# A delta-rule scan on one core: each projection issued in two pieces instead of four

## Chip, cores and metric

One core of one Trainium2 chip runs the whole program. The metric is device time in microseconds, the median of the runs shown. Lower is better. All data is float32.

## What is computed

The program is a pair of transformer-like blocks over 512 tokens of width 1024. The part at issue is the first block's RWKV-7 mixer: the input is projected, shifted along time by three taps, turned into per-head quantities, and scanned forward and backward with a delta rule, first over 256 context tokens, then over the 512 tokens themselves. Cut to that part, the reference is:

```python
z = h @ p["w_in"]
r, k_f, k_b, v, d_f, d_b, kk, a_f, a_b, dg = rwkv_prep(centred_shift(z_rwkv, p["shift_conv"]), p)

def centred_shift(z, w):
    zp = jnp.pad(z, ((0, 0), (1, 1), (0, 0)))
    return zp[:, :-2] * w[0] + zp[:, 1:-1] * w[1] + zp[:, 2:] * w[2]

def step(S, inp):                                  # rwkv_scan, 16 heads of 64
    r_t, k_t, v_t, d_t, kk_t, a_t = inp
    s_kk = jnp.einsum('bhvk,bhk->bhv', S, kk_t)
    S_new = (S * d_t[:, :, None, :] - s_kk[..., None] * (kk_t * a_t)[:, :, None, :]
             + v_t[..., None] * k_t[:, :, None, :])
    y = jnp.einsum('bhvk,bhk->bhv', S if reverse else S_new, r_t)
    return S_new, y
```

After it come the rest of the mixer (merge), a mixture-of-experts layer, and a second block. They take some two thirds of the time and are not touched.

## The kernel before

`stage_scan` (L552) works on eight column groups j = 0..7 of 128 columns, that is two heads each. The scan is chunked: 12 steps of 64 tokens (4 of the context, 8 of the tokens), both directions side by side. Each step needs the inverse of a triangular matrix; the inverses are made in three groups s = 0, 1, 2 of four steps, each by LEVELS = 5 levels l of block doubling. All engines' orders are written out by hand and run in order; semaphores tie them together. The outer loop is over turns j = -1..8. In a turn the engines make the inverses of column group j, run the sequential steps of j (and in s = 0 those last four of j-1), and in the time left prepare the column group b = j+1 and finish a = j-1.

One level (s, l) of a turn on PE, L1083 to L1105, is in this order:

- product (L810, beside it read-outs of values L959, keys L933, or turned tokens L795): DVE then makes the mask (L1445) of its result
- if l < 4, the right side of a step (L904, L908): ACT then negates it (`negate`, L1173)
- half-slot 0: `beside(j, (s, l, 0))`
- if l < 4, the solve (L920), which waits for the negation. ACT then copies U (`solved`, L1179)
- the correct (L880, L882), which waits for the mask; at l = 4 correct_last (L862, L865) stands instead. DVE then updates X and XT (L1456, L1458)
- if l < 4, the read out (L945), which waits for the copy of U. DVE then makes the next state (L1471, L1475)
- half-slot 1: `beside(j, (s, l, 1))`. The next level's product waits for the update.

Each half-slot is named by three numbers, (s, l, 0) or (s, l, 1). `beside` on PE, L1000 to L1078, says which work of b or a goes into each. ACT, DVE have such functions too, with the same names of slots: on ACT the work of half-slot 0 stands between the negation and the copy of U, on DVE that of half-slot 0 between mask and update, that of half-slot 1 behind the state.

`project(j, which, piece)` (L694) makes one of four projections of a column group, by matmuls from `hT` and the weights in `first_chunk`, into one PSUM bank, PROJ: K_X (keys of the tokens), K_V (keys and values of the context, two outputs of 256 columns, L710), R_X and V_X (512 columns, L714), each summed over eight blocks c of 128 rows. A projection is cut into four pieces: two blocks c of 512 columns, or four of 256. In the trace a float32 matmul has two records, so a piece shows as x4 (L714) or x8 (L710). PROJ is one bank: a projection waits until DVE's `shift` (L1484, three operations, at L376, L379, L382 for X and from L1500 on for the context) has read the one before, and the shift of each waits for its last piece (semaphore `proj`).

Work of ACT that stands in half-slots 0 and matters here: at (1,0,0) tokens and `deviation` (L1287, L1292) of column a; at (1,3,0) tokens and `part_moved` (L1229); at (2,0,0) tokens and `blend` (L1259); at (2,3,0) `part_moved` and `exponents` (L1266 to L1270). On DVE: `shift(b, K_X)` at (0,2,1), K_V at (1,1,1), R_X at (2,1,0), V_X at (2,4,1), the last followed by `scaled_q`; `unit_k` (L1553) at (2,0,1). GpSimd (POOL) has `new_k` (L1391 to L1393) after the blend.

Of the kernel before, what the change touches and what calls it, by code (L numbers as in the profile page):

```python
# [12 lines left out]
T, TC, D = 512, 256, 1024  # L13
TA = T + TC
KT = D // P
# [536 lines left out]
def stage_scan(k, hT, th, da, sg, ya, spare, m, first_chunk, first_loaded):  # L552
# [20 lines left out]
    with ExitStack() as s:  # L573
# [40 lines left out]
        Y, RU, INV, INVT, PROJ = (bank[i] for i in range(5))  # L614
# [22 lines left out]
        K_X, K_V, R_X, V_X = range(4)  # L637
# [22 lines left out]
        def _(pe):  # L660
# [33 lines left out]
            def project(j, which, piece):  # L694

                if not live(j):
                    return
                if piece == 0:
                    if which == K_X:
                        pe.wait_ge(S["wk_loaded"], 16 * (j + 1))  # L700
                    elif which == R_X:
                        pe.wait_ge(S["wr_loaded"], 16 * (j + 1))
                    elif which == K_V:
                        pe.wait_ge(S["wv_loaded"], 16 * (j + 1))
                    if proj_no(j, which) > 1:
                        pe.wait_ge(S["shift"], shift_no(j, which - 1) if which else shift_no(j - 1, V_X))
                if which == K_V:
                    i, o = (1, PROJ[:, 0:TC]) if piece < 2 else (2, PROJ[:, TC:2 * TC])
                    for c in range(4 * (piece % 2), 4 * (piece % 2) + 4):
                        last = mm(o, wj[:, c, i, :], hT[:, c, T:TA], start=(c == 0), stop=(c == KT - 1))  # L710
                else:
                    i = {K_X: 1, R_X: 0, V_X: 2}[which]
                    for c in range(2 * piece, 2 * piece + 2):
                        last = mm(PROJ[:], wj[:, c, i, :], hT[:, c, 0:T], start=(c == 0), stop=(c == KT - 1))  # L714
                if piece == 3:
                    last.then_inc(S["proj"], 1)

            def squares(j):
# [20 lines left out]
            def cumulate(j, t):  # L739

                if not live(j):
                    return
                if t == 0:
                    sc.settled(pe, "decay", j, 2)
                    sc.settled(pe, "decay", j, 1)
                    sc.settled(pe, "decay", j, 0)
                o = sc.take(pe, "cum", j, t)
                for d in range(2):
                    if t < NC_:
                        tile = NX + t if d == 0 else NT - 1 - t  # L750
                    else:
                        tile = t - NC_ if d == 0 else NT - 1 - t
                    last = mm(o[:, 2 * P * d:2 * P * d + 2 * P], sig[:, d, tile, :], m["cum"][:, d].rearrange("p i t -> p (i t)"),
                              start=True, stop=True)
                sc.fill(last, "cum", j, t)
# [218 lines left out]
            def variance(j):  # L974
                if not live(j):
                    return
                sc.settled(pe, "center", j)
                o = sc.take(pe, "var", j)
                for t in range(NX):
                    for g in range(0, P, 32):  # L980
                        last = mm(o[g:g + 32, 2 * t:2 * t + 2], ysq[:, t * P + g:t * P + g + 32], k.head_ones[:, ::HEAD],
                                  start=True, stop=True, skip_group_check=True)
                sc.fill(last, "var", j)
# [16 lines left out]
            def beside(j, at):  # L1000

                a, b = j - 1, j + 1
                if at == (0, 0, 0):
                    turn_params(b)
                if at == (0, 0, 1):
                    project(b, K_X, 0)
                if at == (0, 1, 0):
                    project(b, K_X, 1)
                    bonus(j)
                if at == (0, 1, 1):  # L1010
                    project(b, K_X, 2)
                if at == (0, 2, 0):
                    project(b, K_X, 3)
                    scores(j, 4)
                if at == (0, 2, 1):
                    scores(j, 5)
                    scores(j, 6)
                if at == (0, 3, 0):
                    scores(j, 7)
                    rates(b, 0)  # L1020
                if at == (0, 3, 1):
                    rates(b, 1)
                    rates(b, 2)
                    to_tokens(j, "B", 0)
                if at == (0, 4, 0):
                    to_tokens(j, "K", 0)
                    decays(b, 0)
                if at == (0, 4, 1):
                    center(a)
                    decays(b, 1)  # L1030
                    decays(b, 2)
                    project(b, K_V, 0)
                if at == (1, 0, 0):
                    variance(a)
                    project(b, K_V, 1)
                if at == (1, 0, 1):
                    project(b, K_V, 2)
                if at == (1, 1, 0):
                    project(b, K_V, 3)
                    spread_rstd(a)  # L1040
                    gate(a)
                if at == (1, 2, 0):
                    scores(j, 8)
                    scores(j, 9)
                if at == (1, 2, 1):
                    scores(j, 10)
                    scores(j, 11)
                if at == (1, 3, 0):
                    project(b, R_X, 0)
                    squares(b)  # L1050
                if at == (1, 3, 1):
                    project(b, R_X, 1)
                if at == (1, 4, 1):
                    project(b, R_X, 2)
                if at == (2, 0, 0):
                    project(b, R_X, 3)
                    spread_inverse(b)
                if at == (2, 0, 1):
                    cumulate(b, 0)
                if at == (2, 1, 0):  # L1060
                    cumulate(b, 1)
                if at == (2, 1, 1):
                    cumulate(b, 2)
                if at == (2, 2, 0):
                    cumulate(b, 3)
                if at == (2, 2, 1):
                    scores(b, 0)
                    scores(b, 2)
                    cumulate(b, 4)
                if at == (2, 3, 0):  # L1070
                    cumulate(b, 5)
                    project(b, V_X, 0)
                if at == (2, 3, 1):
                    project(b, V_X, 1)
                if at == (2, 4, 0):
                    project(b, V_X, 2)
                if at == (2, 4, 1):
                    project(b, V_X, 3)  # L1078

            BESIDE = {(0, 0): ("V", 0), (1, 0): ("V", 1), (1, 1): ("B", 1), (1, 2): ("K", 1), (1, 3): ("V", 2), (1, 4): ("B", 2),  # L1080
                      (2, 0): ("K", 2)}
# [2316 lines left out]
```

## Time and profile before

| | us |
|---|---|
| median of 3 runs | 3272.14 |
| lowest, highest | 3271.3, 3289.57 |
| profiled execution, first to last instruction (its span) | 3273.4 |
| scan stage within the span | about 105 to 1030 |
| PE busy in the span | 2892.6 (88%) |

The profiled execution's time outside its span isn't listed apart; the median of the runs shown lies 1.3 us below the span. Times in rows are us from the span's start. Engines: PE = TensorE matmul, DVE = VectorE, ACT = ScalarE, POOL = GpSimd. A busy time of PE is that of pipelined matmuls, whose ends overlap the next start by some 0.07 us.

### The profile page before, as it was taken

Reading aid. Unit: us, or ns where it says so; the run is one execution under the profiler, and the core shown is the slowest. Engines: PE = TensorE matmul, PEld = TensorE weight load, DVE = VectorE, ACT = ScalarE, POOL = GpSimd, SP = SyncE. Lnnn points to the kernel's source line nnn. Section 1 sums busy time; section 2 is a strip of 40 time slices with the busy share of each in tenths; the row PEclk is TensorE's granted clock in tenths of the full one; section 3 lists DMA queues with packets and bytes.
Section 4 is the critical chain, followed back from the end, with each engine's and each line's share of the span. In section 5 each row is a group of like instructions: output and inputs, shape, how many; then the busy total and the mean of one; then the engine's idle time right before and its main releaser. Section 6 shows DMA issues by size and latency. Waiting matters only on the chain. (4 is left out here: it accounts for less than half of the span.)

```text
span 3273.4 us, 70453 instructions
## 1 busy us (share of the span) xinstructions
PE 2892.6 (88%) x31462; PEld 1613.2 (49%) x31462; DVE 1155.9 (35%) x2601; ACT 637.7 (19%) x1424; POOL 261.3 (8%) x294
## 2 busy tenths in 40 slices
PE   4799999999987999986988988988987996899987
PEld 2477677767775444434333333333433544455543
DVE  2345554555452773145021122022003435223332
ACT  1233333334331010001000000000002453022230
POOL 1111221122010000001000000000000121010000
PEclk8899999999996999997999999999998997899988
DMA  4100000000001874216999999999993110132202
GB/s 166 40 22 12 23 23 21 12 24 19 11 30 72 285 272 145 77 68 257 431 428 431 429 432 430 431 431 430 431 426 95 52 42 17 63 68 58 58 23 84
DMA packets 192369, 561.75 MB, mean 172 GB/s; under 512 B 32477, under 2 KB 120051, under 8 KB 167511
## 3 DMA queue, kind: packets, MB, share of 16 engines
q1 hardware_dynamic: 192054, 557.45, 43.4%
q8 instruction: 239, 3.92, 0.5%
q14 instruction: 44, 0.35, 0.0%
q10 hardware_dynamic: 32, 0.03, 0.0%
HBM read 554.84 MB, written 2.27 MB: 170 GB/s over the span
## 5 line engine op out<-in xcount | busy, mean ns | idle before, releaser
L2146 PE MATMUL bank<-ex_ring,xe 128*64 128x512 f32 x864 | 332.3, 617 | 39.7 <-DMA ex_ring<-in_exp_w_dram 14.9
L2146 PE MATMUL bank<-mixer_w,xe 128*64 128x512 f32 x576 | 193.7, 600 | 19.2 <-DMA ex_ring<-in_exp_w_dram 9.1
L714 PE MATMUL bank<-hT,first_chunk 128*128 128x512 f32 x384 | 197.7, 642 | 5.6 <-DVE vj L1506 3.0
L2146 PEld LDWEIGHTS bank<-ex_ring,xe 128*64 128x64 f32 x864 | 103.3, 142 | 167.5 <-issue 162.6
L3109 PE MATMUL bank<-h2T_mixer,mixer_w 128*128 128x512 f32 x384 | 176.9, 609 | 2.7 <-PEq L78 2.7
L2146 PE MATMUL bank<-ex_ring,hidT 128*64 128x512 f32 x448 | 169.2, 594 | 2.1 <-DMA h2T_mixer<-in_exp_w_dram 1.9
L2146 PE MATMUL bank<-h2T_mixer,xe 128*64 128x512 f32 x304 | 143.9, 629 | 17.1 <-DMA mixT<-in_exp_w_dram 16.3
L2146 PE MATMUL bank<-mixT,xe 128*64 128x512 f32 x304 | 145.7, 636 | 14.1 <-DMA ex_ring<-in_exp_w_dram 13.3
L2689 PE MATMUL bank<-h2T_mixer,mixer_w 128*128 128x512 f32 x320 | 146.7, 608 | 12.9 <-ACT mixT L2787 8.1
L1445 DVE TENSOR_TENSOR pm<-bank,m_level 128x512 f32<-128x512 f32 x120 | 82.7, 689 | 158.8 <-PE bank L810 157.9
L880 PE MATMUL bank<-pm,XT 64*64 64x32 f32 x3072 | 110.9, 224 | 27.7 <-DVE pm L1445 27.6
L2360 DVE TENSOR_TENSOR x<-x,bank 128x512 f32<-128x512 f32 x64 | 43.7, 686 | 246.0 <-PE bank L2184 246.0
L880 PEld LDWEIGHTS bank<-pm,XT 64*64 64x64 f32 x3072 | 103.7, 141 | 33.8 <-DVE pm L1445 32.9
L1173 ACT ACTIVATE x<-bank 64x128 f32<-64x128 f32 x192 | 52.2, 272 | 312.8 <-PE bank L908 292.3
L882 PE MATMUL bank<-XT,pm 64*64 64x32 f32 x3072 | 113.0, 225 | 0.0
L3109 PEld LDWEIGHTS bank<-h2T_mixer,mixer_w 128*128 128x128 f32 x384 | 71.0, 193 | 84.2 <-issue 84.2
L2146 PEld LDWEIGHTS bank<-mixer_w,xe 128*64 128x64 f32 x576 | 61.8, 138 | 99.6 <-issue 96.4
L2538 PE MATMUL bank<-po_w,mixT 128*128 128x512 f32 x256 | 110.7, 594 | 0.0
L810 PE MATMUL bank<-X,px 64*64 64x64 f32 x2560 | 98.5, 228 | 10.9 <-DVE XT L1458 10.0
L810 PEld LDWEIGHTS bank<-X,px 64*64 64x64 f32 x2560 | 86.6, 140 | 41.9 <-issue 23.3
L2353 DVE TENSOR_TENSOR hid<-sil,bank 128x512 f32<-128x512 f32 x32 | 19.8, 682 | 245.4 <-PE bank L2146 245.4
L2689 PEld LDWEIGHTS bank<-h2T_mixer,mixer_w 128*128 128x128 f32 x320 | 60.5, 195 | 87.7 <-issue 78.9
(511 smaller groups left out, 5603.1 us busy)
## 6 DMA issues: line engine op xcount, KB each, us to landing
ex_ring<-in_exp_w_dram SPq DMA_DIRECT2D x82, 2048.0 KB, 22.9
mixer_w<-in_exp_w_dram SPq DMA_DIRECT2D x54, 2048.0 KB, 23.1
h2T_mixer<-in_exp_w_dram SPq DMA_DIRECT2D x28, 2048.0 KB, 21.9
mixT<-in_exp_w_dram SPq DMA_DIRECT2D x28, 2048.0 KB, 22.0
ws_w<-in_ada_w_dram SPq DMA_DIRECT2D x40, 1024.0 KB, 5.2
mixer_w<-in_odd_w_in_dram SPq DMA_DIRECT2D x32, 512.0 KB, 3.9
first_chunk<-in_w_in_dram SPq DMA_DIRECT2D x24, 512.0 KB, 3.9
mixer_w<-in_even_w_in_dram SPq DMA_DIRECT2D x24, 512.0 KB, 4.0
```

The costliest lines, as they stand in the source:

```text
L714: last = mm(PROJ[:], wj[:, c, i, :], hT[:, c, 0:T], start=(c == 0), stop=(c == KT - 1))
L810: last = mm(INV[c, cs(q)], part(4 * g + q // 2, q % 2, 0, 0)[h], X[h, (j * GROUPS + g) % 2, q, :], start=True, stop=True)
L880: mm(into(INV, h, q), XT[c, g, q, :], blocks(pm[c, q, :], b, 0), start=True, stop=True)
L882: last = mm(into(INVT, c, q), pm[c, q, :], blocks(XT[c, g, q, :], b, 1), start=True, stop=True)
L1173: last = f(rn[c], RU[h, 0:P].rearrange("p (d v) -> p d v", d=2), ACT.Copy, scale=-1.0)
L1445: tt(pm[:], INV[:].rearrange("p (q t) -> p q t", q=8), m["level"][:, l, :].unsqueeze(1).to_broadcast([P, 8, HEAD]), ALU.mult).then_inc(S[" ...
L2146: r[e] = mm(out[a, :], lhs[j][:, a], w[:, j, 512 * c:512 * c + 512], start=(first and j == 0), stop=(last and j == len(lhs) - 1), skip_gro ...
L2353: dve.tensor_tensor(hid[:, f, :], sil[:, f, :], bank[4 + f][:], ALU.mult).then_inc(S["hid_made"], 1)
L2360: dve.tensor_tensor(x1[:, n, c], x1[:, n, c], bank[scatter_bank(q, o)][:], ALU.add).then_inc(S["added"], 1)
L2538: last = pe.matmul(bank[i % 6][:], mixT[:, j, n * P:n * P + P], w[:, h, j, :], start=(j == 0), stop=(j == KT - 1))
L2689: last = mm(o[:], w[:, c, i, :], hT[:, i, :], start=(i == 0), stop=(i == KT - 1))
L3109: last = mm(o[:], w[:, i, t, :], hT[:, t, :], start=(t == 0), stop=(t == KT - 1))
```

## The change

Each projection is issued in two pieces of twice the length: four blocks c of 512 columns, or all eight of 256. In the order on PE, eight half-slots of a turn lose a piece and eight get one twice as long:

| projection | pieces before | pieces after |
|---|---|---|
| K_X | (0,0,1) (0,1,0) (0,1,1) (0,2,0) | (0,0,1) (0,1,1) |
| K_V | (0,4,1) (1,0,0) (1,0,1) (1,1,0) | (0,4,1) (1,0,1) |
| R_X | (1,3,0) (1,3,1) (1,4,1) (2,0,0) | (1,3,1) (1,4,1) |
| V_X | (2,3,0) (2,3,1) (2,4,0) (2,4,1) | (2,3,1) (2,4,0) |

No instruction of ACT, DVE, POOL or SyncE is moved.

```diff
                 if which == K_V:
-                    i, o = (1, PROJ[:, 0:TC]) if piece < 2 else (2, PROJ[:, TC:2 * TC])
-                    for c in range(4 * (piece % 2), 4 * (piece % 2) + 4):
+                    i, o = (1, PROJ[:, 0:TC]) if piece == 0 else (2, PROJ[:, TC:2 * TC])
+                    for c in range(KT):
                         last = mm(o, wj[:, c, i, :], hT[:, c, T:TA], start=(c == 0), stop=(c == KT - 1))
                 else:
                     i = {K_X: 1, R_X: 0, V_X: 2}[which]
-                    for c in range(2 * piece, 2 * piece + 2):
+                    for c in range(4 * piece, 4 * piece + 4):
                         last = mm(PROJ[:], wj[:, c, i, :], hT[:, c, 0:T], start=(c == 0), stop=(c == KT - 1))
-                if piece == 3:
+                if piece == 1:
                     last.then_inc(S["proj"], 1)
...
                 if at == (1, 0, 0):
                     variance(a)
+                if at == (1, 0, 1):
                     project(b, K_V, 1)
-                if at == (1, 0, 1):
-                    project(b, K_V, 2)
```

PE around the half-slot (1,0,0), before: keys (L933), right side (L904), variance (L981), piece (L710), solve (L920), correct (L880, L882).

```order
L933 MATMUL bank<-x,tokK 64x64 x4
L904 MATMUL bank<-x,pc 64x64 x4
L981 MATMUL bank<-head_ones,ysq 32x2 x16
L710 MATMUL bank<-hT,first_chunk 128x256 x4
L920 MATMUL bank<-x,XT 64x64 x4
L880 MATMUL bank<-pm,XT 64x32 x2
L882 MATMUL bank<-XT,pm 64x32 x2
```

The same place after:

```order
L933 MATMUL bank<-x,tokK 64x64 x4
L904 MATMUL bank<-x,pc 64x64 x4
L981 MATMUL bank<-head_ones,ysq 32x2 x16
L920 MATMUL bank<-x,XT 64x64 x4
L880 MATMUL bank<-pm,XT 64x32 x2
L882 MATMUL bank<-XT,pm 64x32 x2
```

The four matmuls of 256 columns between the variance and the solve are gone; they stand in half-slot (1,0,1), behind the read out.

PE around the half-slot (2,4,0), before: end of the product (L959, L810), piece of V_X (L714), correct_last (L862, L865).

```order
L959 MATMUL bank<-px,x 64x64 x2
L810 MATMUL bank<-X,px 64x64 x4
L714 MATMUL bank<-hT,first_chunk 128x512 x2
L862 MATMUL bank<-XT,pm 64x32 x2
L865 MATMUL bank<-m_id,XT 64x64 x2
```

The same place after:

```order
L959 MATMUL bank<-px,x 64x64 x2
L810 MATMUL bank<-X,px 64x64 x4
L714 MATMUL bank<-hT,first_chunk 128x512 x4
L862 MATMUL bank<-XT,pm 64x32 x2
L865 MATMUL bank<-m_id,XT 64x64 x2
```

The piece ahead of correct_last has twice the matmuls.

PE at the end of a turn, before: end of correct_last, last piece of V_X in (2,4,1), then the next turn's first product with turned tokens (L810, L795).

```order
L862 MATMUL bank<-XT,pm 64x32 x2
L865 MATMUL bank<-m_id,XT 64x64 x2
L714 MATMUL bank<-hT,first_chunk 128x512 x2
L810 MATMUL bank<-X,pc 64x64 x2
L795 MATMUL bank<-m_id,vj 64x64 x2
```

The same place after:

```order
L862 MATMUL bank<-XT,pm 64x32 x2
L865 MATMUL bank<-m_id,XT 64x64 x2
L810 MATMUL bank<-X,pc 64x64 x2
L795 MATMUL bank<-m_id,vj 64x64 x2
L810 MATMUL bank<-X,pc 64x64 x2
```

Between correct_last and the product that reads its result nothing stands any more.

## Rows read from the trace of the kernel before

**Rows 1.** The page: the span, and the first row of busy time by engine.

```profile
span 3273.4 us, 70453 instructions
...
PE 2892.6 (88%) x31462; PEld 1613.2 (49%) x31462; DVE 1155.9 (35%) x2601; ACT 637.7 (19%) x1424; POOL 261.3 (8%) x294
```

**Rows 2.** Windows: stretch, length, busy us of each engine, granted clock, DMA share, GB/s.

```profile
105.00:1030.00 925.00, 856.06 (x22317) 652.81 (x22319) 456.63 (x974) 307.56 (x749) 154.87 (x120) 0.96 0.07 20
...
488.00:598.00 110.00, 104.11 (x2824) 78.93 (x2827) 57.54 (x124) 38.86 (x95) 19.26 (x15) 1.00 0.07 20
```

**Rows 3.** Waits of PE in the scan: us in total, times, longest.

```profile
PE bank L880 <- DVE pm L1445: 27.6, 27, 3.7
...
PE bank L945 <- ACT x L1179: 1.5, 3, 0.7
```

**Rows 4.** Timeline, level (1,0) of turn 3: start, us, engine, line; ACT, then PE.

```profile
529.44 0.56 ACT L1173 ACTIVATE x<-bank 64x128 f32<-64x128 f32 x2 [2.70 <-PE bank L904]
...
530.63 1.28 ACT L1292 ACT_TABLE_LOAD   x1
...
532.11 0.28 ACT L1179 ACTIVATE x<-bank 128x128 f32<-128x128 f32 x1
...
529.69 1.99 PE L710 MATMUL bank<-hT,first_chunk 128*128 128x256 f32 x8
531.61 0.39 PE L920 MATMUL bank<-x,XT 64*64 64x64 f32 x6
...
532.75 0.42 PE L945 MATMUL bank<-x 64*64 64x64 f32 x7
```

**Rows 5.** Timeline, level (1,3) of turn 3: ACT, then PE.

```profile
553.47 1.27 ACT L1229 ACTIVATE XT<-px 64x512 f32<-64x512 f32 x2
...
552.14 1.98 PE L714 MATMUL bank<-hT,first_chunk 128*128 128x512 f32 x4
...
555.70 0.42 PE L945 MATMUL bank<-x 64*64 64x64 f32 x7
```

**Rows 6.** Timeline of PE: the bonus in (0,1,0), the spread of rstd in (1,1,0).

```profile
499.73 1.02 PE L966 MATMUL bank<-rkr,head_r_k 128*128 128x512 f32 x2
...
538.65 1.05 PE L991 MATMUL bank<-ident,ysq 128*128 128x128 f32 x8
```

**Rows 7.** Timeline, level (2,0) of turn 3: ACT, then PE.

```profile
565.90 1.66 ACT L1259 ACTIVATE kt<-ra,pcol 128x1536 f32<-128x1536 f32 x1
...
569.10 0.42 PE L945 MATMUL bank<-x 64*64 64x64 f32 x7
```

**Rows 8.** Timeline, level (2,3) of turn 3: ACT, then PE.

```profile
588.30 0.19 ACT L1270 ACTIVATE eh<-bank 128x4 f32<-128x4 f32 x1
...
589.52 0.42 PE L945 MATMUL bank<-x 64*64 64x64 f32 x7
```

**Rows 9.** Timeline from (2,4) of turn 3 to (0,0) of turn 4: DVE, then PE.

```profile
595.95 0.42 DVE L1458 TENSOR_TENSOR XT<-XT,bank 128x256 f32<-128x256 f32 x1 [0.29 <-PE bank L862]
597.90 0.75 DVE L376 TENSOR_SCALAR vj<-bank,pcol 128x512 f32<-128x512 f32 x1 [1.52 <-PE bank L714]
...
602.61 0.25 PE L880 MATMUL bank<-pm,XT 64*64 64x32 f32 x2 [1.86 <-DVE pm L1445]
```

**Rows 10.** Timeline, (2,0) and (2,1) of turn 3: DVE, then POOL.

```profile
570.57 0.97 DVE L1475 TENSOR_TENSOR ZG<-Z,g 128x128 f32<-128x128 f32 x1
...
575.45 0.42 DVE L1456 TENSOR_TENSOR X<-X,bank 128x256 f32<-128x256 f32 x1
...
569.41 0.74 POOL L1392 TENSOR_TENSOR kt<-kt,kj 128x256 f32<-128x256 f32 x1
```

**Rows 11.** Timeline, end of turn -1: DVE, then POOL.

```profile
156.45 1.75 DVE L1586 TENSOR_TENSOR qr<-rj,qr 128x512 f32<-128x512 f32 x1
...
157.61 2.80 POOL L1402 TENSOR_TENSOR kt<-kt,bt 128x1024 f32<-128x1024 f32 x1
```

**Rows 12.** The window behind the start of turn 5, and a K piece in turn 6.

```profile
713.90:717.30 3.40, 3.40 (x8) 0.87 (x7) 1.10 (x5) 0.00 (x0) 0.00 (x0) 0.50 0.03 7
...
825.85 3.78 PE L714 MATMUL bank<-hT,first_chunk 128*128 128x512 f32 x4
```

More of the change, by code:

```diff
@@ L1007, in beside @@
                 if at == (0, 1, 0):
-                    project(b, K_X, 1)
                     bonus(j)
                 if at == (0, 1, 1):
-                    project(b, K_X, 2)
+                    project(b, K_X, 1)
                 if at == (0, 2, 0):
-                    project(b, K_X, 3)
                     scores(j, 4)
@@ L1034, in beside @@
                     variance(a)
+                if at == (1, 0, 1):
                     project(b, K_V, 1)
-                if at == (1, 0, 1):
-                    project(b, K_V, 2)
                 if at == (1, 1, 0):
-                    project(b, K_V, 3)
                     spread_rstd(a)
@@ L1048, in beside @@
                 if at == (1, 3, 0):
-                    project(b, R_X, 0)
                     squares(b)
                 if at == (1, 3, 1):
+                    project(b, R_X, 0)
+                if at == (1, 4, 1):
                     project(b, R_X, 1)
-                if at == (1, 4, 1):
-                    project(b, R_X, 2)
                 if at == (2, 0, 0):
-                    project(b, R_X, 3)
                     spread_inverse(b)
@@ L1071, in beside @@
                     cumulate(b, 5)
+                if at == (2, 3, 1):
                     project(b, V_X, 0)
-                if at == (2, 3, 1):
+                if at == (2, 4, 0):
                     project(b, V_X, 1)
[L1075 to L1078, printed above, removed]
             BESIDE = {(0, 0): ("V", 0), (1, 0): ("V", 1), (1, 1): ("B", 1), (1, 2): ("K", 1), (1, 3): ("V", 2), (1, 4): ("B", 2),
```

## Prediction, made before the changed kernel was run

> **What bounds the kernel now.** I read the page first: TensorE (PE) is busy 88% of 3273.4 us, far more than any other engine [rows 1]. The windows come next: the scan lies in 105 to 1030 us, with PE busy 856.06 of 925.00 us, and one steady turn, 488 to 598, has 104.11 of 110.00 [rows 2]. So in the scan the matmul stream sets the time, and only some 6 us of a turn are idle PE. After the scan nothing that the change touches runs, and the expert weights are not loaded ahead of its end, so what a turn loses goes to the end in full. The waits of PE say who ends the idle time: above all the mask on VectorE (DVE), 27.6 us over 27 waits, while ScalarE's (ACT) copy of U ends 1.5 us over 3 [rows 3]. Then I read one turn, engine by engine, in order of time.
>
> A level of a turn on PE is: product, right side, half-slot 0, solve, correct, read out, half-slot 1. Each gap between them covers a round trip: the solve waits for ACT's negation, the correct for DVE's mask, the read out for ACT's copy of U, which stands in ACT's own order behind whatever ACT does in half-slot 0. So a piece in a half-slot is both work and cover.
>
> **The change, part by part.** A piece holds PE for about 1.91 us: the V/K piece begins at 529.69 and the solve behind it at 531.61, and pieces of both shapes are busy for 1.98 or 1.99 [rows 4, 5]. A piece of twice the length is 3.82. Eight half-slots of a turn lose 1.91 each, eight gain 1.91 each, the sum of matmuls is the same. In the half-slots that grow, all 1.91 are added, since one piece already outlasted the round trip there. So the question is in which of the eight emptied half-slots PE does not get its 1.91 back.
>
> Three give it back in full. At (0,1,0) the bonus matmul stays, 1.02 us, at (0,2,0) the eight scores of 128 columns, at (1,1,0) the spread of rstd, 1.05, and the gate behind it; the negation needs 0.56 [rows 4, 6], and they run beside it. I cost these at 0; if the negation outlasts the scores it costs 0.2. ACT has little behind its negation there.
>
> (1,0,0): only the variance stays. ACT, after the negation (529.44 to 530.00), copies tokens, loads a table (530.63, 1.28 us), takes the root and only then copies U, at 532.11 for 0.28, so to 532.39 [rows 4]. None of this waits for the piece: the variance matmuls stood ahead of it. The read out began at 532.75 and can begin at 532.44: 0.31 back of 1.91, 1.60 lost.
>
> (1,3,0): the squares stay. ACT moves a part from 553.47 to 554.74 whatever PE does, then copies U, 0.28 as above: the read out can begin at 555.09 against 555.70 [rows 5]: 0.61 back, 1.30 lost.
>
> (2,0,0): ACT's blend ends at 567.56, the copy of U follows: read out at 567.92 against 569.10 [rows 7]: 1.18 back, 0.73 lost.
>
> (2,3,0): the last exponent ends at 588.49, copy of U to 588.78, read out at 588.83 against 589.52 [rows 8]: 0.69 back, 1.22 lost.
>
> (2,4,1): the last V piece goes ahead of correct_last, which so ends 1.91 later, its update (595.95, 0.42) too, at 598.28. DVE's shift of V is behind this update in its order and cannot use that V is ready earlier: it starts at 598.31 against 597.90. From there to the mask of the next turn's first level DVE is the chain, and PE waits for it, 1.86 us today [rows 9]. So +0.41. The idle time there only changes its place: a wait of some 0.8 behind correct_last, for ACT's copy of X, is new, and the one before the mask gets shorter.
>
> One thing comes back. After (2,0) DVE is late: L1475 takes 0.97 us, since it meets POOL's three multiplications of new_k, then come unit_k, the mask, the shift of R, and the update of (2,1) at 575.45 [rows 10]. With the read out 1.18 earlier, L1475 would be asked at some 568.9, while POOL is in the first of the three, since the second began at 569.41. L1475 alone needs 0.3, and ended at 571.54. If it slips in between the first and the second, as DVE's L1586 of the first turn did between two of POOL (it was over at 158.20, while POOL's L1402 stood from 157.61 to 160.41 [rows 11]), it ends near 569.8, and all behind it on DVE is free to move by up to 1.7. The mask of (2,1) then waits a little for its product, and the update of (2,1) moves 1.65 us, not 1.18: 0.47 back. If it waits for all three, mask and update stay where they are, and of 1.18 nothing comes back: 1.65 more lost per turn. I take the first, being the one that has a row, and keep the second for the range.
>
> That row agrees with what the Trainium skill says (SBUF — State Buffer, "Who interferes with whom"): a DVE operation with two SBUF inputs and a GpSimd one hold the shared port by turns, each for a whole instruction. By that rule the sum is the one with 0.47 back; a lock over a burst would make it 1.65 x 7 = 12 us more.
>
> Sum for a turn: 1.60 + 1.30 + 0.73 + 1.22 + 0.41 - 0.47 = 4.8 us. Turns 0 to 6 have such pieces beside work. Turn -1 has them nearly back to back, with nothing to cover, so 0 (at most 0.8, for the X copy behind the last V piece); turns 7 and 8 have none. Turn 0 lacks the variance and gate of a column before: I count it as the rest. 7 x 4.8 = 34 us. Against the profiled execution's span that is 3273.4 + 34 = 3307; the median of the runs shown is 3272.14, 1.3 below the span, so by it 3306. To this I add about 1 us for the clock (below): 3307, 1.07% above.
>
> **The clock.** The granted clock is half (1.2 GHz of 2.4) in the stretch 713.90 to 717.30, right behind the idle stretch of the turn's beginning (the last of its waits is 1.86 in a turn like it [rows 9]), and a K piece behind another such wait, at 825.85, took 3.78 us instead of 1.98 [rows 12]. It happened at some turns' beginnings, not at all. Each time it costs about 1.8. The change shortens the longest wait there a little but adds four holes of 0.5 to 1.0 us elsewhere, all beside wide matmuls. Nearest rows are the holes that exist today without a lower clock, as those of 488 to 598, granted 1.00 [rows 2]. Bounds: one less in all, or one more in each turn, -2 to +13 us; I take +1.
>
> The Trainium skill (TensorE: Matmul & The Clock Gate, "HAM oscillation — how this bites in real kernels") has the rule that gaps in PE's work bring the lower clock back, and it speaks against this change. By it every turn could pay once more; the sum would then be 3307 + 13. The trace agrees where the hole is long (the row at 713.90) and shows none for the short ones.
>
> **Rivals.**
> 1. ACT does not hold the read out: what stays in the slots is cover enough, and only the negation counts. Then (1,0,0) loses 0.35 (solve at 530.05, behind the negation, instead of 1.91 ahead of 531.61), (1,3,0) some 0.2 by the same reckoning, (2,0,0) and (2,3,0) nothing, plus 0.41, less 0.47: 0.5 us a turn, 3.6 in all, 3276, no change. For it: the emptied slots all keep a matmul group of 0.4 to 2 us. Against: ACT runs in order, and its rows show the copy of U following L1292, L1229, L1259 and L1270 closely or with at most 0.9 us between [rows 4, 5, 7, 8]. It decides if in these four slots U's copy can start before that work ends. This is the case that ends as not slower.
> 2. The new holes bring the half clock at each turn: 7 x 1.8 = 13 more, 3320. For it: rows 12. Against: the holes are shorter than the 1.86 that did it, and even that one did not in every turn.
> 3. DVE waits for the whole POOL burst at (2,0): 1.65 x 7 = 12 more, 3318.
> 4. Longer runs of one shape save something at their seams. A piece takes 1.98 with 0.07 of it beside the next, so no seam is seen; four seams less for each projection could give 0.3 us a turn at most, 2 us; 3305, inside the forecast's own range.
>
> **How the numbers follow.** Forecast (with its own range 3298 to 3314, from the roundings of the six terms, 0.1 to 0.2 each, and a clock stretch or two) 0.58, rival 1 0.14, rival 2 0.15, rival 3 0.10, something else 0.03. From no change, a measurement here can tell about 1%, which is 3305: the forecast lies just above it, so 0.21 of its 0.58 falls within 1%. Within 1%: 0.14 + 0.21 + 0.01 = 0.36; slower by over 1%: 0.37 + 0.15 + 0.10 = 0.62; faster by over 1%: 0.02, for what I have not seen. The range is 3286 to 3324: it takes in rivals 2 and 3 singly, and leaves out rival 1's end and both of them together.
>
> **What would show it.** In the profile after: a turn that is 4.8 us longer (from one L1445 of level (0,0) to the next), 34 over the stage; new waits of PE's L945 on ACT's L1179 of some 1.0, 0.9, 0.5 and 0.8 us in the levels (1,0), (1,3), (2,0), (2,3) (the correct then ends that long before the copy of U does), about 22 us in all where there are 1.5 today [rows 3]; the busy time of L714 and L710 unchanged; L1475 of (2,0) over by 569.8 on today's scale; the wait of L880 at (0,0) about as today. Wrong if L945 waits for nothing (rival 1), if L714 takes more than today's busy time by 10 us (rival 2), or if L1475 at (2,0) grows to over 2 us (rival 3).

## The result, and the profile of the changed kernel

The median went from 3278.12 us (3271.3 to 3289.57, 4 runs) to 3311.34 us (3306.18 to 3317.1, 4 runs): a ratio of 1.0095, 95% interval 1.0071 to 1.012. That is 33.2 us more. The forecast was 35 more (34, and 1 for the clock), 3307, with a range of 3286 to 3324. The time is in the range, and the interval leaves no doubt that the kernel is slower; but 0.95% is just inside what I had called no change, and I had given slower by over 1% the most.

The number came out and its parts did not. First the page, its span and first row of busy time:

```profile
span 3304.5 us, 70453 instructions
...
PE 2909.6 (88%) x31462; PEld 1623.5 (49%) x31462; DVE 1167.3 (35%) x2601; ACT 634.5 (19%) x1424; POOL 255.3 (8%) x294
```

The same instructions in a span that is 31.1 longer [rows 1]. Next the windows, cut at the first product matmul of turn 0, that of turn 7, and the scan's last correct; columns as in [rows 2]. The kernel before:

```profile
161.30:931.10 769.80, 726.77 (x19394) 549.07 (x19393) 398.15 (x850) 266.69 (x648) 136.84 (x107) 0.99 0.07 18
931.10:1021.60 90.50, 74.08 (x2522) 67.29 (x2522) 39.38 (x90) 22.39 (x57) 6.22 (x5) 0.77 0.08 28
```

The changed one:

```profile
164.00:971.80 807.80, 747.13 (x19393) 567.56 (x19393) 409.61 (x850) 263.72 (x648) 130.53 (x107) 0.97 0.06 17
971.80:1050.60 78.80, 63.10 (x2524) 56.42 (x2526) 38.91 (x90) 22.28 (x57) 6.20 (x5) 0.94 0.09 30
```

So of 31.1 us, +38.0 lie in turns 0 to 6, -11.7 in turn 7, +2.7 ahead of the scan's turns and +2.1 behind the scan. The granted clock splits the first: read slice by slice, turns 0 to 6 have 20.4 us at half clock before and 51.0 now. Half of the difference, 15.3, is the clock's, if all of it is matmul time; 22.7 remain, 3.2 a turn. In turn 7 it is the other way: 41.5 us at half clock before (granted 0.77), 10.2 now (0.94), and no piece stands in that turn at all. These are one profile of each kernel, and the runs of the kernel before alone lie 18 us apart; so what the clock does in turn 7 can't be put down to the change.

The waits of PE, from 105 us to 1065:

```profile
PE bank L880 <- DVE pm L1436: 21.6, 18, 3.1
PE bank L945 <- ACT x L1170: 14.5, 28, 1.0
PE bank L920 <- ACT x L1164: 12.5, 24, 0.7
...
PE bank L810 <- ACT X L1226: 6.4, 9, 0.7
PE bank L880 <- issue: 3.8, 6, 1.3
```

DVE's, ACT's and POOL's line numbers are 9 lower here than in [rows 3 to 10], PE's are the same. The second row is the wait that I had forecast: 1.5 us over 3 waits before [rows 3], 14.5 over 28 now, where I had said 22. In turns 0 to 6 there are 23: six at (1,0), 1.01 in four of them and less in two; three at (1,3), up to 0.72; seven each at (2,0), of 0.17, and at (2,3), of 0.69 but for one. The fourth is the new wait for ACT's copy of X, 0.71 each, the "some 0.8" of my step on (2,4,1). The last one I had not seen coming: PE idle among the small matmuls of the correct, with no semaphore in the profile that it waits for. Four of the six stand at (1,3), in turns 0, 1, 2 and 6, where the wait for ACT is missing, and two at (1,0).

The timeline of turn 2 has three of the four places. Level (1,0), ACT, then PE, against [rows 4]:

```profile
437.09 1.28 ACT L1283 ACT_TABLE_LOAD   x1
...
438.55 0.27 ACT L1170 ACTIVATE x<-bank 128x128 f32<-128x128 f32 x1
...
436.50 0.39 PE L920 MATMUL bank<-x,XT 64*64 64x64 f32 x6 [0.29 <-ACT x L1164]
438.87 0.45 PE L945 MATMUL bank<-x 64*64 64x64 f32 x8 [1.01 <-ACT x L1170]
```

The table load, the root and the copy of U run one behind the other, and the read out starts 0.32 behind the copy's start, as I had worked out (532.11 and 532.44 in the prediction); before, it started 0.64 behind, since the piece held it. At (2,0) and at (2,3), against [rows 7] and [rows 8]:

```profile
476.62 0.27 PE L945 MATMUL bank<-x 64*64 64x64 f32 x1 [0.17 <-ACT x L1170]
496.07 0.45 PE L945 MATMUL bank<-x 64*64 64x64 f32 x8 [0.69 <-ACT x L1170]
```

Behind (2,0), DVE and then POOL, against [rows 10]:

```profile
478.22 0.29 DVE L1466 TENSOR_TENSOR ZG<-Z,g 128x128 f32<-128x128 f32 x1
...
476.48 1.81 POOL L1382 TENSOR_TENSOR kt<-kt,kj 128x768 f32<-128x768 f32 x1 [12.91 <-ACT kt L1250]
478.25 0.85 POOL L1383 TENSOR_TENSOR kt<-kt,kj 128x256 f32<-128x256 f32 x1
```

DVE's multiplication starts where the first one of POOL ends and takes 0.29 in place of 0.97. This is the one turn in which it comes so late; in the other six of turns 0 to 6 it starts 1.22 behind the start of POOL's first, takes 0.74 (0.95 to 0.97 before), and is over 0.15 after that first one has ended. So it waits for the first alone and not for all three, as forecast; by the rows it then overlaps the second, which takes 0.78 to 0.85 in place of 0.74. And the seam of turns 2 and 3, DVE, then PE, against [rows 9]:

```profile
505.95 0.42 DVE L1449 TENSOR_TENSOR XT<-XT,bank 128x256 f32<-128x256 f32 x1 [1.83 <-PE bank L862]
506.29 0.75 DVE L376 TENSOR_SCALAR vj<-bank,pcol 128x512 f32<-128x512 f32 x1
...
506.66 0.27 PE L810 MATMUL bank<-X,pc 64*64 64x64 f32 x2 [0.72 <-ACT X L1226]
511.00 0.25 PE L880 MATMUL bank<-pm,XT 64*64 64x32 f32 x2 [1.38 <-DVE pm L1436]
```

The idle time moved from before the mask (1.86, now 1.38) to before the product (0.72).

What a piece is worth shows in three rows. A double piece of turn 2 at full clock, and one of turn 3 at half clock:

```profile
461.47 3.70 PE L714 MATMUL bank<-hT,first_chunk 128*128 128x512 f32 x8
...
512.33 5.40 PE L714 MATMUL bank<-hT,first_chunk 128*128 128x512 f32 x8
```

Eight matmuls take 3.70, four took 1.98 [rows 5]: the second four are worth 1.72, not the 1.91 that I used.

Last, where the clock falls. Two windows of 3.4 us in the changed kernel's turn 3, at its start and at level (1,0):

```profile
512.40:515.80 3.40, 3.40 (x4) 1.41 (x5) 1.24 (x5) 0.00 (x0) 0.00 (x0) 0.50 0.03 9
553.40:556.80 3.40, 3.25 (x14) 2.69 (x15) 1.38 (x5) 0.73 (x2) 0.00 (x0) 0.50 0.00 0
```

Before, the stretches in turns 0 to 6 began behind the seam alone, at (0,0), in four turns (twice 3.4 us, twice 6.8). Now they begin at (0,0) in six turns, at (1,0) in three and at (1,3) in four. Levels (1,0) and (1,3) are two of the four with a new hole.

To compare turns without the clock, I take from here on for each part of a level (product to correct, correct to next product) the difference to the kernel before in turns where neither kernel has half clock there. Clean means that, and the figures are medians over turns 0 to 6; a stall of PE that the kernel before doesn't have is left in unless I say so.

### The profile page after: what moved, and what is told of

It is laid out like the page before. It is cut to its first block and busy times, and to the rows that moved or that the text cites. A ratio compares the mean times of both kernels' runs of the same rounds, so it can differ in the third digit from the quotient of the medians.

```text
span 3304.5 us, 70453 instructions
## 1 busy us (share of the span) xinstructions
PE 2909.6 (88%) x31462; PEld 1623.5 (49%) x31462; DVE 1167.3 (35%) x2601; ACT 634.5 (19%) x1424; POOL 255.3 (8%) x294
## 5 line engine op out<-in xcount | busy, mean ns | idle before, releaser
L2137 PE MATMUL bank<-ex_ring,xe 128*64 128x512 f32 x864 | 339.9, 629 | 39.0 <-DMA ex_ring<-in_exp_w_dram 14.4
L2137 PE MATMUL bank<-mixer_w,xe 128*64 128x512 f32 x576 | 199.0, 611 | 19.6 <-DMA mixer_w<-in_exp_w_dram 10.1
L714 PE MATMUL bank<-hT,first_chunk 128*128 128x512 f32 x384 | 196.6, 661 | 2.5 <-DMA first_chunk<-in_w_in_dram 2.5
L880 PE MATMUL bank<-pm,XT 64*64 64x32 f32 x3072 | 109.5, 222 | 26.3 <-DVE pm L1436 21.6
L714 PEld LDWEIGHTS bank<-hT,first_chunk 128*128 128x128 f32 x384 | 77.2, 211 | 88.0 <-issue 82.3
L880 PEld LDWEIGHTS bank<-pm,XT 64*64 64x64 f32 x3072 | 101.4, 139 | 31.1 <-DVE pm L1436 28.2
L882 PE MATMUL bank<-XT,pm 64*64 64x32 f32 x3072 | 112.9, 224 | 0.0
L810 PE MATMUL bank<-X,px 64*64 64x64 f32 x2560 | 94.8, 223 | 9.2 <-DVE XT L1449 8.4
```

The source lines that it names most:

```text
L810: last = mm(INV[c, cs(q)], part(4 * g + q // 2, q % 2, 0, 0)[h], X[h, (j * GROUPS + g) % 2, q, :], start=True, stop=True)
L880: mm(into(INV, h, q), XT[c, g, q, :], blocks(pm[c, q, :], b, 0), start=True, stop=True)
L882: last = mm(into(INVT, c, q), pm[c, q, :], blocks(XT[c, g, q, :], b, 1), start=True, stop=True)
L2137: r[e] = mm(out[a, :], lhs[j][:, a], w[:, j, 512 * c:512 * c + 512], start=(first and j == 0), stop=(last and j == len(lhs) - 1), skip_gro ...
```

## The experiments

My theory after the first result: a turn pays the four lost covers and the seam, some 3.1 us clean; the rest of the scan's time is clock, set off by holes. The rivals: double length costs something by itself (the stalls in the correct); or it is the emptied half-slot, whatever ACT does.

**act_late** is the changed kernel with ACT's work that stood ahead of U's copy put behind it:

```diff
-                if at == (1, 0, 0):
+                if at == (1, 0, 1):
                     tokens(j, "V", 1)
                     deviation(a)
...
-                if at == (1, 3, 0):
+                if at == (1, 3, 1):
                     tokens(j, "V", 2)
                     part_moved(j, 2)
...
-                if at == (2, 0, 0):
+                if at == (2, 0, 1):
                     tokens(j, "K", 2)
                     blend(b)
...
-                if at == (2, 3, 0):
+                if at == (2, 3, 1):
                     part_moved(b, 0)
                     exponents(b, 5)
```

> Two pieces as in the change, but ACT's work of half-slots (1,0,0), (1,3,0), (2,0,0) and part_moved and exponents of (2,3,0) stands in half-slot 1, behind the copy of U. Theory (ACT's order holds the read out in these four levels): the waits of L945 on the copy of U, 14.5 us in 28 waits in the changed kernel, fall to under 3 us, a turn gets about 3 us shorter without the clock, the time is 0 to 10 us above the kernel before instead of 33. Rival (the length of the pieces itself costs, or only the clock does): it stays 20 us or more above.

3290.97 us against 3279.29, ratio 1.0032 (1.0013 to 1.005): of the 33 us, some 21 are gone; 11.7 stay, a little over the 0 to 10 that I had expected. Its waits of PE:

```profile
PE bank L880 <- issue: 5.8, 6, 1.5
...
PE bank L945 <- issue: 1.8, 2, 1.4
```

In turns 0 to 6 L945 waits for ACT no more, and a clean turn, with the stalls left out, is 0.4 us shorter than before. So the lost covers are ACT's order in front of the copy of U; the empty half-slots 0 cost nothing in a turn that the clock and the stalls leave alone. What stays lies in the clock (30.6 us of turns 0 to 6 at half clock, 10.2 more than before) and in the stalls (all of PE's waits for issue in turns 0 to 6 are 9.3 us, before 0.9).

**fill** is the changed kernel with fillers, four matmuls of 128x512 in the trace, in each of the four half-slots (1,0,0), (1,3,0), (2,0,0), (2,3,0). Their result is not used; nothing of the computation is left out.

```diff
+            def filler(j):
+                if live(j):
+                    for c in range(2):
+                        mm(INVT[:], hT[:, c, 0:P], hT[:, c, 0:T], start=True, stop=True)
```

> The changed kernel with two idle matmuls of 512 columns (1.7 us, result unused) added in the half-slots (1,0,0), (1,3,0), (2,0,0), (2,3,0) of turns -1 to 6, 55 us of TensorE work in all. Theory (there are holes of 1.26, 0.99, 0.42 and 0.93 us there, and half-clock stretches behind them): the holes take 3.6 of the 6.9 us of a turn, so +30 over the changed kernel, and up to 12 less where half-clock stretches behind these holes go: +18 to +30. Rival (TensorE has no hole there, its work alone sets the time): +50 or more.

3320.37 against 3279.29, 1.0146 (1.0104 to 1.0188): 41 us above the kernel before, where the changed kernel is 33 above it. These 8 us are less than the 18 to 30 that I had expected, though 128 matmuls were added, which follow each other at 0.43 (1.72 by four): 55 us. The waits for ACT are filled, and so is something else: no stretch of half clock lies at (1,0) or (1,3) any more, 13.6 us in all in turns 0 to 6 instead of 51.0. That is the first sign that these stretches come from the holes. Clean, a turn is 3.7 us longer than in the changed kernel, 26 in seven; the clock gives back 19 of it, more than the 12 that I had allowed.

**two_half0** puts double pieces into the four half-slots 0 and leaves half-slots 1 empty:

```diff
                 if at == (1, 0, 0):
                     variance(a)
+                    project(b, K_V, 1)
-                if at == (1, 0, 1):
-                    project(b, K_V, 1)
...
```

and the same for R_X 0 at (1,3,0), R_X 1 at (2,0,0), V_X 0 at (2,3,0).

> Two pieces per projection, but placed in the half-slots 0 where ACT has work: K_V 1 at (1,0,0), R_X at (1,3,0) and (2,0,0), V_X at (2,3,0) and (2,4,0). Empty are now half-slots 1 behind a read out: (1,0,1), (1,3,1), (1,4,1), (2,3,1), where TensorE waits only for DVE's update; their slack in the kernel before is 1.22, 1.21, 1.41 and 1.21 us of a piece's 1.72. Theory (a piece's value is the cover it gives where it stands): each loses 0.3 to 0.5, some 1.9 us a turn, 13 us above the kernel before, and fewer half-clock stretches than the changed kernel. Rival (two pieces of double length cost by themselves): as the changed kernel, 30 us or more above.

3297.82 against 3279.29, 1.0059 (1.0037 to 1.0081): 18.5 us above, between the 13 of the theory and the 30 of the rival. An empty half-slot 1 gives back 1.13 to 1.17 of 1.72 and loses 0.57 each time, beside 0.93 to 1.43 for three of the four half-slots 0 in the changed kernel. So the doubling is cheaper with the other half-slot emptied, and not free. Turns 0 to 6 have 34.1 us at half clock, fewer than in the changed kernel as expected; ten of them are at (2,0) and (1,4), where no other kernel has any.

**bonus_score** keeps four pieces and moves two small things one or two half-slots earlier:

```diff
                 if at == (0, 0, 0):
+                    bonus(j)
                 if at == (0, 1, 0):
                     project(b, K_X, 1)
-                    bonus(j)
...
                     scores(j, 9)
+                    scores(j, 10)
                 if at == (1, 2, 1):
-                    scores(j, 10)
                     scores(j, 11)
```

> The kernel before (four pieces) with the bonus matmul moved from (0,1,0) to (0,0,0) and the scores of step 10 from (1,2,1) to (1,2,0), where TensorE waits 1.86 and about 1.1 us for the mask. Theory (idle TensorE before a late mask takes other work for nothing): 1.0 + 0.8 us a turn, 8 turns, 13 us below the kernel before, and some half-clock stretches less, up to 10 us more. Rival (the mask gets later by as much, since DVE waits for what is moved): no change.

3259.66 against 3279.29, 0.9929 (0.9903 to 0.9956): faster, by 19.6 us. The clean parts of (0,1) and (1,2) are 0.86 and 0.55 shorter. It is the same arithmetic the other way round: work that stands where nothing waits is put where PE waits for DVE.

**One projection at a time.** Four kernels, each the kernel before with one projection in two pieces:

```diff
-            def project(j, which, piece):
+            def project(j, which, piece, of=4):
...
-                    project(b, K_V, 0)
+                    project(b, K_V, 0, of=2)
...
```

(Here the lines of K_V; in all four `project` takes its share of the blocks from `of`.)

> Only K_X in two pieces, the other three in four as before. Theory (what stays at (0,1,0) and (0,2,0) is cover enough): a turn without half-clock stretches stays within 0.3 us of the kernel before (in the changed kernel these levels came to -0.2). Rival (each emptied half-slot costs some): +1 us a turn or more.

> Only K_V in two pieces. Theory: the hole at (1,0), since the copy of U stands behind the deviation on ACT: 1.4 us a turn without clock, 10 us in seven turns, 7 waits of L945 on ACT of up to 1.0 us, and some half-clock stretches that begin at (1,0), none at (1,3). Rival: no hole, under 3 us in all.

> Only R_X in two pieces. Theory: holes at (1,3) of 1.0 and (2,0) of 0.4 us, 0.6 regained at (2,1) and (2,2): 0.8 us a turn without clock; the stalls inside the corrects at (1,3), for which no instruction waits in the program and which are in the changed kernel (3.8 us) and not before, are seen here too, and half-clock stretches at (1,3). Rival for these stalls (they come from what is doubled at (0,4,1) and (1,0,1)): they are in kv_two and not here.

> Only V_X in two pieces. Theory: a hole of 0.9 us at (2,3), and 0.1 from (2,4) to the mask of (0,0): 1.0 us a turn without clock, 7 us in seven turns; 7 waits of L945 on ACT. Rival (the shift of V, ready earlier, wins time at (0,0)): no slower, or faster.

Each ran once, so their times tell little (3288.23, 3281.05, 3281.87 and 3293.2, beside 3289.88 of the kernel before on that chip); the clean turns tell more:

| projection | clean, us a turn | its parts |
|---|---|---|
| K_X | -0.17 | at (0,2) |
| K_V | +1.43 | (1,0) |
| R_X | +0.77 | (1,3) +0.99, (2,0) +0.42, (2,1) and (2,2) -0.63 |
| V_X | +1.04 | (2,3) +0.93, (2,4) and the next (0,0) +0.11 |

They sum to 3.07, and the changed kernel has 3.08 by the same reckoning: the parts add up, and times 7 they are 21.6 of the 22.7. The waits agree. For K_V, R_X and V_X alone, one fence each:

```profile
PE bank L946 <- ACT x L1178: 7.0, 10, 1.0
```

```profile
PE bank L881 <- issue: 3.9, 4, 1.4
PE bank L946 <- ACT x L1178: 4.3, 12, 0.7
```

```profile
PE bank L811 <- ACT X L1233: 6.4, 9, 0.7
PE bank L946 <- ACT x L1177: 6.6, 11, 0.7
```

(Lines are 1 higher on PE.) The same wait in the kernel before is 1.9 in this longer window. The stalls in the correct at (1,3) come with R_X, which empties (1,3,0), and with no other. Of the six in the changed kernel four are there; the other two, of 0.5 and 0.7, are at (1,0), which K_V empties, and kv_two has one of 0.4 there. On the clock the four tell something that I had not expected: kv_two makes the hole at (1,0), 1.0 us long, and has every stretch of half clock at (0,0), none at (1,0); rx_two has two at (1,3). A hole of 1.0 us does not bring one by itself. And kx_two, which has no new hole, has 37.5 us at half clock in turns 0 to 6, all at (0,0), more than the kernel before; it was profiled once.

**q_late** takes one operation out of the chain at the seam: the second scaling of q waits one slot, so that DVE comes to the mask sooner.

```diff
                 if at == (0, 0, 0):
+                    scaled_q(j, 1)
                     params(b)
                 if at == (2, 4, 1):
-                    scaled_q(b, 1)
```

> The kernel before with DVE's scaled_q of the tokens moved from (2,4,1), ahead of the next turn's first mask, to (0,0,0), behind it. Theory (from (2,4) to (0,0) DVE is the chain and TensorE waits 1.86 + 0.49 us for it): the mask is 1.75 us earlier, 1.5 to 1.75 us a turn, 8 turns, -12 to -14 us, and fewer half-clock stretches at turns' starts. Rival (what is moved delays the update of (0,0), or the scores at (0,2,0)): no change.

3250.59 against 3272.2, 0.9923 (0.9897 to 0.9949), 21.6 us below where I had expected 12 to 14: a clean (0,0) is 1.61 shorter, and only 6.8 us of turns 0 to 6 are at half clock.

**best** is the kernel before, four pieces, with bonus_score and q_late together.

> q_late and bonus_score together: bonus at (0,0,0), scores of step 10 at (1,2,0), scaled_q behind the first mask. Theory (fill the holes that DVE leaves): 1.5 + 0.86 + 0.55 us a turn at best, -18 to -24 us without the clock against the kernel before, and with the half-clock stretches at turns' starts gone some 8 us more. Rival (the moves want the same hole): no more than the better one of the two.

3235.96 (6 runs, 3229.68 to 3247.58) against 3272.2, 0.9893 (0.9869 to 0.9918): faster than both kernels. Its windows, turns 0 to 6 and turn 7, and its wait for the mask:

```profile
161.80:902.80 741.00, 718.97 (x19394) 544.76 (x19393) 393.05 (x850) 266.99 (x648) 133.07 (x107) 1.00 0.07 19
902.80:981.10 78.30, 62.21 (x2525) 56.08 (x2526) 38.83 (x90) 22.35 (x57) 5.69 (x5) 0.96 0.09 32
```

```profile
PE bank L880 <- DVE pm L1445: 4.9, 17, 1.4
```

The wait that led [rows 3], 27.6 us, is 4.9. The turns are 3.0 us shorter clean, 21 in seven, and the 20.4 us at half clock, which cost some 10 before, are gone: 31 by this reckoning, 28.8 by the windows. Turn 7 is 12 us shorter in this profile as well (78.3), with less half clock, as in the changed kernel.

**hole_fill** is the kernel before with the same filler, result not used, ahead of the mask at (0,0,0) alone.

> The kernel before with two idle matmuls of 512 columns (1.7 us, result unused) in the half-slot (0,0,0) of turns 0 to 7, where TensorE waits 0.49 and 1.86 us; 14 us of TensorE work added, none taken away. Theory (the half-clock stretches at turns' starts come from this hole): turns without such a stretch stay as long as before within 0.2 us, the stretches at (0,0) of turns 1 to 6 (13.6 us of half clock in the profile of before) are gone, the time is 0 to 10 us below the kernel before. Rival (the stretches come from something else): they stay, and the time is the same or up to 14 us above.

3264.6 against 3277.02, 0.9954 (0.994 to 0.9968). Turns 0 to 6:

```profile
162.20:923.80 761.60, 732.12 (x19426) 550.48 (x19425) 398.18 (x850) 267.15 (x648) 136.87 (x107) 1.00 0.07 18
```

Some 14 us of useless matmuls (32 at 0.43) make the kernel faster. Turns 0 to 6 hardly differ from those of the kernel before that had no half clock, since the filler lies in the wait for the mask; granted 1.00 instead of 0.99. So the stretches behind the seam come from the hole in front of the mask, and filling it or closing it takes them away: hole_fill, best and two_best have none at (0,0) in turns 0 to 6, q_late one in turn 0, the other ten kernels three to seven.

**two_best** is the changed kernel with q_late, the earlier score and act_late: the best that I know for two pieces. The bonus matmul, which best has moved too, stays at (0,1,0).

> Two pieces per projection as in the changed kernel, with ACT's work behind the copy of U (act_late), scaled_q behind the first mask (q_late) and the scores of step 10 at (1,2,0). Theory (the pieces' length is free once nothing needs their cover): act_late stands at -0.4 us a turn against before without clock and stalls, q_late gives 1.6, the scores 0.55 less what (1,3) gives back: some 2.3 us a turn, -16 us, within 10 us of the best four-piece kernel, the stalls inside the corrects at (1,3) still there. Rival (double length costs by itself): at least 20 us behind it.

3271.11 (10 runs) against 3277.02, 0.9978 (0.9955 to 1.0001): the expectation failed. It is 5.9 us below the kernel before, where best, on another chip, is 36.2 below it: some 30 behind best, not within 10. Two rows of its waits:

```profile
PE bank L880 <- issue: 5.6, 8, 1.2
...
PE bank L862 <- issue: 3.2, 3, 2.1
```

By the windows it loses 24.5 us to best in turns 0 to 6 (765.5), 5.1 in turn 7, 4.1 ahead and 6.8 behind. Of the 24.5 the clock is 5.1 (10.2 us, all at (1,3)). PE's waits for issue in turns 0 to 6, of all its lines, are 13.0 against 2.7 in best, so at most 10.3 more; the three of L862 above lie behind turn 6. And the bonus move, which two_best lacks, is worth 0.86 a turn in best, 6.0 in seven. Some 3 have no name. So once ACT is out of the way, double pieces cost little or nothing in a clean turn. What two_best loses beside the bonus lies nearly all in stalls and in half clock at (1,3); L880's stalls and the half clock there are found only in kernels with an emptied (1,3,0). That double length costs nothing by itself is still not shown for the whole.

## Why the prediction was right in its number and wrong in its parts

**A piece is 1.91 us.** Wrong by 0.19. Removed and added it moves the clean parts by 1.72, and 3.70 less 1.98 is the same. I took the distance from one group's start to the next, which holds 0.19 that stays where it is when the piece goes. Each lost cover is smaller by that.

**The three free half-slots.** Right: (0,1,0), (1,1,0) nothing, (0,2,0) -0.17.

**The four lost covers.** The mechanism was right: L945 waits behind ACT's queue at exactly these levels, and with ACT's work behind the copy the waits are gone. The sizes, forecast and measured: (1,0,0) 1.60 and 1.43, (1,3,0) 1.30 and 0.99, (2,0,0) 0.73 and 0.42, (2,3,0) 1.22 and 0.93. With 1.72 for the piece my working gives 1.41, 1.11, 0.54 and 1.03, within 0.12 of each. That is the mis-sized term, 1.1 us a turn: 0.76 of it is the length of the piece four times over.

**The seam.** Forecast +0.41, measured +0.11: the mask's wait shrank from 1.86 to 1.38 while the product's grew by 0.72. My list of signs had this wait "about as today", against my own step that it gets shorter; the step was right.

**What comes back at (2,1).** Forecast 0.47, measured 0.63. DVE's L1475 waited for POOL's first operation and not for all three, as I had said, so rival 3 fell. By the Trainium skill (SBUF — State Buffer, "Who interferes with whom") a DVE operation with two SBUF inputs contends with a GpSimd one that reads SBUF. The traces agree: 0.74 us for the operation that met POOL's first, 0.29 for the one that came at its end, 0.97 for the one before that met the third.

**The sum for a turn.** Forecast 4.8, measured 3.1: 21.6 us in seven instead of 34.

**The clock.** I had taken +1, with +13 as rival 2. In turns 0 to 6 it was +15.3: rival 2 came true, though not as I had put it: nine slices of 3.4 us more, two of them at the seam, three at (1,0) and four at (1,3). The rule of the Trainium skill (TensorE: Matmul & The Clock Gate, "HAM oscillation — how this bites in real kernels"), that gaps in PE's work bring the lower clock back, pointed the right way. The page states it for gaps longer than the new holes are; in the changed kernel idle spots of 0.4 to 1.4 us had half clock behind them. What stood against that in the total was turn 7, -11.7, which I had not priced at all and which one profile can't tie to the change. Forecast 34 + 1; measured 21.6 + 15.3 - 11.7 + 2.7 + 2.1 and 1.1 unnamed, 31.1. The number is right in part by luck: the turns' sum without the clock came out 12.4 below mine, the clock 14.3 above it, turn 7 11.7 below, the rest 5.9 above, -3.9 together. In the whole span both profiles have a granted clock of 0.948.

**My test for rival 2 was blind.** I had said that L714's busy time would grow by 10 us if the clock fell. For turns 0 to 6, the kernel before, then the changed one:

```profile
L714 PE MATMUL bank<-hT,first_chunk 128*128 128x512 f32 x337 | 173.0, 637 | 0.0
```

```profile
L714 PE MATMUL bank<-hT,first_chunk 128*128 128x512 f32 x336 | 170.2, 653 | 0.0
```

The busy time fell while the mean of one matmul rose from 637 to 653 ns. Each run of a shape has one end of some 0.26 us that lies beside the next group (1.98 less 1.72); half as many runs have half as many ends, which took away what the clock added. The mean, or the granted clock by slices, is what shows it.

**Still open.** What decides where a stretch of half clock falls: hole_fill and best show that filling or closing the hole at the seam ends those behind it, kv_two that a hole of 1.0 us at (1,0) brings none there while the changed kernel, with the same hole and others, has three. Those at (1,3) were seen in the changed kernel, act_late, rx_two and two_best alone, the same four that stall in the correct; but neither brings the other each time, since the changed kernel has the stretch without a stall in turns 4 and 5, behind a wait of 0.72 for ACT, and the stall without a stretch in turns 1 and 2. What decides how long turn 7 is at half clock, which puts its length between 78 and 92 us: it is 31 us or more in the kernel before, bonus_score, vx_two and hole_fill, 17 at most in the others, and I see nothing that the first four share and the others lack. What would keep the stalls in the correct away other than wide matmuls. And of two_best against best the last 3 us of turns 0 to 6, and 7 more behind the scan.

## What to carry to other kernels

Before work is taken out of a gap, read what the gap's end waits for and what stands ahead of that on its own engine; here moving ACT's work behind the copy gave back two thirds of the loss, and moving two small matmul groups and one DVE operation in the other direction made it 1.1% faster than the kernel before. Price a group by the difference between a long and a short run of it, not from one start to the next. And look for half clock by slices of the granted clock, never by the busy time of a line, and give idle spots at a turn's seam a price in clock as well as in their length.

## What was new about the hardware

**PE stalls that wait for no semaphore.** In runs of small matmuls of the correct, PE stands still for 0.3 to 1.5 us. The changed kernel, turn 2, in (1,3):

```profile
460.26 0.24 PE L880 MATMUL bank<-pm,XT 64*64 64x32 f32 x1 [0.59 <-issue]
```

By kernel, us and times of L880's waits for issue: 3.8 in 6 for the changed kernel, 5.8 in 6 for act_late, 3.9 in 4 for rx_two, 5.6 in 8 for two_best, none in the kernel before, kx_two, vx_two, bonus_score, q_late and best (0.4 in kv_two, 0.3 in two_half0; 2.3 in 2 in hole_fill, in turn 7). What all of the first four have is a half-slot (1,3,0) without wide matmuls, so that small ones stand in a row from the product to the read out; fill, where that half-slot has wide ones again, has 0.3 at most. Other lines of PE have such waits too, the kernel before one of 0.8 at L904.

That the sequencer runs out of instructions in a long row of small ones is what the traces point to. The page has a DMA queue for instructions, 239 transfers of 16 KB in the kernel before:

```profile
q8 instruction: 239, 3.92, 0.5%
```

173 of them fall in turns 0 to 7, one for each 253 of PE's matmuls and weight loads. Over all fourteen kernels every wait for issue of L880 of 0.3 us or more, 27 in number, ends 1.20 to 1.59 us after such a transfer has landed, and of PE's 113 waits of this kind 98 end 1.1 to 1.6 us after one. A time picked at random in these turns lies that far behind a landing in one case of ten. The one above ends at 460.26; the transfer before it ran from 457.54 to 459.00. So these stalls end with the arrival of instructions; no run here changes the supply to test it.

**Half clock behind short holes.** The granted clock fell to 1.2 GHz behind idle spots of 0.4 to 1.9 us, often two or three close together (3.7 at most, in turn 0), in a stretch in which PE was busy 93% of the time [rows 2], for 3.4 us, sometimes 6.8, and came back by itself. Matmuls that compute nothing, put into the spot at the seam, kept it at 2.4 GHz and paid for themselves (hole_fill); in the four half-slots 0 of the changed kernel they did not (fill).

**Turn 7.** Where no projections stand beside the scan, PE is busy 82% of the turn in the kernel before, and 7 to 48 us of it, from kernel to kernel, are at half clock. The turn takes 78 to 92 us by that. The runs of the one kernel before lie up to 30 us apart, and the longer ones have the lower granted clock: of 14 on one chip the shortest took 3266.05 at 0.952, the longest 3295.82 at 0.942, which makes some 69 us more at half clock. So the half clock differs from run to run of the same code by enough for this. Whether it does so in turn 7 is not shown, since each kernel has one profile.
